# Column sums of the adaptive parameters between matmuls of an up group, and down groups that wait for their activation remainders by halves

## What is computed

```python
# end of the first block: the feed-forward part, D_FF = 2816
hf = rms_norm(x, g_pre_ffn)
f_gate, f_up = jnp.split(hf @ w_ffn_in, 2, axis=-1)
f = (jax.nn.silu(f_gate) * f_up) @ w_ffn_out
return x + rms_norm(f, g_post_ffn)

# start of each layer of the second block: 3072 adaptive parameters
c_act = jax.nn.silu(c)
mod = c_act @ w_ada + b_ada          # (1, 1024) @ (1024, 3072)
shift, scale, gate = jnp.split(mod, 3, axis=-1)
```

## Time and profile before

| | |
|---|---|
| median of 3 runs | 2731.32 us |
| profiled execution, its own time | 2728.5 us |
| its span | 2726.8 us |
| mean granted TensorE clock | 0.983 |
| TensorE busy | 2643.9 us (97%) |
| TensorE weight loads busy | 2217.8 us (81%) |
| VectorE, ScalarE, POOL busy | 1213.8, 965.2 and 410.3 us |

### The profile page before, as it was taken

How to read it: one execution, slowest core, us unless ns; L and a number is a source line. 1 busy time by engine, 2 the same in 40 slices (tenths; PEclk the granted TensorE clock), 3 DMA queues, 4 the chain that set the end, 5 groups by cost and what they waited for, 6 DMA issues and landing times.

```text
span 2726.8 us, 33510 instructions
## 1 busy us (share of the span) xinstructions
PE 2643.9 (97%) x13229; PEld 2217.8 (81%) x13245; DVE 1213.8 (45%) x1645; ACT 965.2 (35%) x1289; POOL 410.3 (15%) x428
## 2 busy tenths in 40 slices
PE   7999999999999999998999999999999999999998
PEld 7887778777888878786888888888888888888887
DVE  5435554744534765634433333443443333343435
ACT  6425454225324412213433332323253333322222
POOL 3104332200000100000301001321021001032300
PEclk9989999999999999999999999999999999999999
DMA  5210003222242554522222223122222222322122
GB/s 202 92 62 17 17 17 105 92 82 78 93 178 85 186 185 151 188 78 93 93 95 100 90 100 113 68 104 77 94 84 101 92 92 98 124 83 94 72 102 76
DMA packets 43592, 269.39 MB, mean 99 GB/s; under 512 B 5128, under 2 KB 5264, under 8 KB 16224
## 3 DMA queue, kind: packets, MB, share of 16 engines
q1 hardware_dynamic: 32080, 227.59, 23.3%
q0 software_dynamic: 11120, 39.27, 4.2%
q10 hardware_dynamic: 288, 1.05, 0.1%
HBM read 265.79 MB, written 2.10 MB: 98 GB/s over the span
## 4 chain that ended last, share of the span: by engine, by line
PE 65%; issue 23%; DVE 6%; POOL 4%; ACT 2%; DMA 1%; DVEq 0%; POOLq 0%; SPq 0%; ACTq 0%
PE PS L1888 63%; DVE w_split L1148 1%; POOL merged L586 1%; PE PS L2113 1%; POOL res_lo L580 1%; POOL res_hi L580 1%; ACT w_split L623 1%; POOL merged L525 1%; DMA raw<-in_weights 1%; DVE small L1446 1%; DVE R L1534 0%; DVE h_act L1156 0%; DVE ks_lo L1383 0%; PE PS L2335 0%; PE PS L1975 0%
## 5 line engine op out<-in xcount | busy, mean ns | idle before, releaser
L1888 PE MATMUL PS<-h_act,w_split 128*128 128x512 f32 (+1 forms) x5856 | 1271.2, 379 | 12.7 <-DVE w_split L1148 3.8
L1888 PEld LDWEIGHTS PS<-h_act,w_split 128*128 128x128 f32 x5856 | 1054.2, 190 | 215.0 <-issue 4.3
L1148 DVE TENSOR_TENSOR w_split<-raw,w_split 128x2048 fp32r<-128x2048 f32 x213 | 504.6, 2369 | 905.0 <-ACT w_split L623 888.2
L623 ACT ACTIVATE w_split<-raw 128x2048 fp32r<-128x2048 f32 x213 | 407.7, 1914 | 824.4 <-PE PS L1888 815.7
L1888 PE MATMUL PS<-w_split,h_act 128*128 128x512 f32 (+1 forms) x1728 | 410.8, 387 | 4.5 <-DVE w_split L1148 3.3
L1888 PEld LDWEIGHTS PS<-w_split,h_act 128*128 128x128 f32 x1728 | 314.1, 190 | 60.2 <-DVE w_split L1148 4.3
L1888 PE MATMUL PS<-y_act,w_split 128*128 128x512 f32 x1152 | 265.4, 391 | 2.2 <-DVE w_split L1148 2.2
L1888 PEld LDWEIGHTS PS<-y_act,w_split 128*128 128x128 f32 x1152 | 217.5, 189 | 47.8 <-DVE w_split L1148 2.6
L1888 PE MATMUL PS<-R 128*128 128x128 f32 (+3 forms) x896 | 190.3, 364 | 9.7 <-ACT R L1041 5.5
L1888 PEld LDWEIGHTS PS<-R 128*128 128x128 f32 x896 | 135.2, 201 | 42.6 <-issue 15.5
L1888 PE MATMUL PS<-w_split,res_hi 128*128 128x384 f32 x512 | 130.9, 336 | 0.0
(11 more groups left out here) (276 smaller groups left out, 2144.9 us busy)
## 6 DMA issues: line engine op xcount, KB each, us to landing
raw<-in_weights SPq DMA_DIRECT2D x213, 1024.0 KB, 4.8
R<-in_w_ada POOLq DMA_DIRECT2D x36, 512.0 KB, 5.0
gate_bc<-in_w_ada POOLq DMA_DIRECT2D x12, 512.0 KB, 4.9
R<-in_nsa_wk POOLq DMA_DIRECT2D x1, 2048.0 KB, 10.3
xres<-in_x POOLq DMA_DIRECT2D x1, 2048.0 KB, 10.8
R<-in_decay POOLq DMA_DIRECT2D x8, 256.0 KB, 3.3
out<-R SPq DMA_DIRECT2D x3, 512.0 KB, 2.6
xres<-in_x ACTq DMA_DIRECT2D x2, 512.0 KB, 4.0
```

Source lines behind the costliest of these rows:

```text
L623: act.activation(w_split[:, 0, half, :, :], raw[:, half, :, :], ACT.Copy).then_inc(w_hi, 1)
L1148: dve.tensor_tensor(w_split[:, 1, half, :, :], raw[:, half, :, :], w_split[:, 0, half, :, :].bitcast(F32), ALU.subtract).then_inc(w_lo, 1)
L1888: return pe.matmul(out, lhsT, rhs, start=start, stop=stop, skip_group_check=True)
```

## The change

A pair of down groups no longer waits for all its remainders first. Its first group waits for those of contraction tiles 0 to 3 ahead of its first half, and for the rest ahead of its second half. This is done in three places (two chunks and the last pair).

The 24 column matmuls of a chunk no longer stand in a block behind the down groups. They stand in the next up group (up group a of the second chunk, and `ffn_up0`), one behind each second matmul from the tenth on: behind matmuls 10, 12, ... 56 of the 96. They write bank 4, of set 1, which that up group does not use; what waits for VectorE's addition is now the up group after it, which uses set 1.

VectorE adds the columns (`ada_columns`) inside that up group, behind its `split_lo` of the next group's first half. Because `ada_acc` must not be written before TensorE has read it, the panel that stood ahead of that group's work now stands behind the addition. VectorE's two loops are now written out by the host, so that places can differ.

```diff
--- before.py
+++ after.py
@@ -172,7 +172,7 @@
     ("w_o", C(g=2, u0=1, u1=1, h=6, l=6)),
     ("norm2", C(u1=1, h=2 * KT, l=2 * KT)),
     ("ffn", 2, [("up", 2, [("a", C(g=1, u0=1, s=2, l=2)), ("b", C(g=1, u1=1, s=2, l=2))]),
-                ("down", C(g=2, u0=1, u1=1)), ("ada", C(u0=1))]),
+                ("down", C(g=2, u0=1, u1=1)), ("ada", C(u1=1))]),
     ("ffn_up0", C(g=1, u0=1, s=2, l=2)),
     ("ffn_up1", C(g=1, u1=1, s=2, l=2)),
     ("ffn_up2", C(g=1, u0=1, s=2, l=2)),
@@ -1626,8 +1626,9 @@
                       lambda part, kts: norm_lo(at("norm2"), V_G2, part, kts))
 
 
-            def up(own, c, S, y0):
+            def up(own, c, S, y0, between=lambda: None):
                 split_lo(c.g + 1, 0)
+                between()
                 for b in range(2):
                     tile = stage[:, 2 * S + b:2 * S + b + 1, :]
                     dve.wait_ge(staged, c.s + b + 1)
@@ -1664,11 +1665,23 @@
             dve.wait_ge(fo_zero, 1)
             dve.wait_ge(cond_ready, 1)
             dve.wait_ge(mod_in, 32)
-            with dve.Fori(0, 2) as ch:
-                with dve.Fori(0, 2) as i:
+            def ada_columns(ch):
+                dve.wait_ge(ada_ps, ch + 1)
+                cols = ada[:, ch:ch + 1, :]
+                dve.tensor_tensor(cols, cols, PS[:, 4:5, 0:ADA_COLS], ALU.add).then_inc(ada_ready, 1)
+                release(1, ada_ready, ch + 1)
+
+            for ch in range(2):
+                for i in range(2):
                     own = Chain(dve, own_ffn, 2 * ch + i, 8 + 2 * KT)
-                    ada_panel(own, ch, 2 * i)
-                    up(own, at("ffn.up.a", ch, i), 0, 4 * i)
+                    if ch and not i:
+                        def columns_panel():
+                            ada_columns(0)
+                            ada_panel(own, 1, 0)
+                        up(own, at("ffn.up.a", ch, i), 0, 4 * i, columns_panel)
+                    else:
+                        ada_panel(own, ch, 2 * i)
+                        up(own, at("ffn.up.a", ch, i), 0, 4 * i)
                     ada_panel(own, ch, 2 * i + 1)
                     up(own, at("ffn.up.b", ch, i), 1, 4 * i + 2)
                     own.end()
@@ -1679,14 +1692,13 @@
                         dve.sem_inc(ada_summed, 1)
                     add_down(at("ffn.down", ch), n, n)
                 own.end()
-                dve.wait_ge(ada_ps, ch + 1)
-                cols = ada[:, bass.ds(ch, 1), :]
-                dve.tensor_tensor(cols, cols, PS[:, 0:1, 0:ADA_COLS], ALU.add).then_inc(ada_ready, 1)
-                release(0, ada_ready, ch + 1)
-            modulation(0)
             own = Chain(dve, own_ffn2)
+
+            def second_columns():
+                ada_columns(1)
+                modulation(0)
             for n in range(3):
-                up(own, at(f"ffn_up{n}"), n % 2, 2 * n)
+                up(own, at(f"ffn_up{n}"), n % 2, 2 * n, lambda: None if n else second_columns())
             own = line
             c = at("ffn_down")
             first_gain, second_gain = [gains[:, GAIN_SLOT["post2"], n * W:(n + 1) * W] for n in range(2)]
@@ -2211,29 +2223,39 @@
             merged_group(c, 24)
             last_group(c.plus(C(g=1)), 0, Hr, at("norm2"), ROWS["norm2"])
             Yr = rows_of(y_act, block_rows)
+
+            def group_with_columns(c, ch):
+
+
+                for n, _ in enumerate(dense(c, 0, H)):
+                    col = n // 2 - 4
+                    if n % 2 == 0 or not 0 <= col < ADA_COLS:
+                        continue
+                    if col == 0:
+                        pe.wait_ge(set_free[1], at("ffn.ada", ch).u1)
+                        pe.wait_ge(ada_summed, ch + 1)
+                    ins = mm(PS[:, 4, col:col + 1], ada_acc[:, col // 4, col % 4 * P:(col % 4 + 1) * P],
+                             cf[:, C_ONE:C_ONE + 1], True, True)
+                    if col == ADA_COLS - 1:
+                        ins.then_inc(ada_ps, 1)
+
             for ch in range(2):
                 for i in range(2):
                     if ch == i == 0:
                         first_group(at("ffn.up.a", 0, 0), at("norm2"), ROWS["norm2"])
+                    elif i == 0:
+                        group_with_columns(at("ffn.up.a", ch, i), ch - 1)
                     else:
                         group(at("ffn.up.a", ch, i), 0, H)
                     group(at("ffn.up.b", ch, i), 1, H)
                 c = at("ffn.down", ch)
-                pe.wait_ge(act_lo, c.l)
-                for n in range(2):
-                    group(c.plus(C(g=n)), n, Yr, feat=False)
-
-                pe.wait_ge(set_free[0], at("ffn.ada", ch).u0)
-                pe.wait_ge(ada_summed, ch + 1)
-                for col in range(ADA_COLS):
-                    last = mm(PS[:, 0, col:col + 1], ada_acc[:, col // 4, col % 4 * P:(col % 4 + 1) * P],
-                              cf[:, C_ONE:C_ONE + 1], True, True)
-                last.then_inc(ada_ps, 1)
-            for n in range(3):
+                group(c, 0, Yr, feat=False, lows=(c.l - 4, c.l))
+                group(c.plus(C(g=1)), 1, Yr, feat=False)
+            group_with_columns(at("ffn_up0"), 1)
+            for n in (1, 2):
                 group(at(f"ffn_up{n}"), n % 2, H)
             c = at("ffn_down")
-            pe.wait_ge(act_lo, c.l)
-            group(c, 1, Yr, feat=False, kph=(4, 2))
+            group(c, 1, Yr, feat=False, kph=(4, 2), lows=(c.l - 2, c.l))
             last_group(c.plus(C(g=1)), 0, Yr, at("layer.norm", 0), ROWS["layer"], kph=(4, 2))
 
 
```

## The result

| | before | changed |
|---|---|---|
| median, first comparison | 2730.34 us (4 runs, 2726.47 to 2734.41) | 2710.69 us (4 runs, 2709.37 to 2712.84) |
| profiled execution | 2728.5 us | 2711.64 us |
| its span, mean clock | 2726.8 us, 0.983 | 2709.9 us, 0.986 |

The ratio is 0.9929, with a 95% interval from 0.9911 to 0.9946. On 2730.34 us that is 19.4 us less, 14.7 to 24.3. The forecast was 2714.9 us: 16.4 less than the 2731.3 that it set out from, and 15.4 less than this median.

What follows compares the result with a forecast made beforehand. TensorE, busy 97% of the span, was taken to bound the kernel. Removing 6.46 + 16.00 + 4.88 = 27.3 us and adding 10.9 saves 16.4, so 2731.3 becomes 2714.9 us; range 2708 to 2724.

Steps and rivals of the forecast that it cites:

- The entry waits: TensorE's three waits for `y_act` at the entries of down group pairs; all 2.21 + 2.20 + 2.05 = 6.46 us goes.
- The blocks and the clock behind them: Two column blocks behind down groups: 16.00 us removed, plus 4.88 us lost to the lowered clock in wide matmuls behind.
- The price of a column: Columns among wide matmuls of the up groups: 0.226 us each, 10.9 us added in all.
- the lower bound of 0.107: Columns in the up groups: one exposed weight load each, 0.107 us, or 5.1 us added in all.
- The loops: VectorE's loops written out: they save VectorE its branch and add none on TensorE; 0 us.
- VectorE's timetable: Up group with columns, from its start T: next group's weight halves ready at T + 19.7 and about T + 32.5.
- The slack at the second: Next group's second weight half: ready at about T + 32.5, wanted at T + 38.1, T being the column group's start.
- A: Up groups with columns: the clock falls there too, 10.3 us lost in all, gain 6.1, 2725.2 us; chance 0.08.
- B: Down groups still wait at entry for hidden weights or banks; gain 9.9 us, 2721.4 us; chance 0.06.
- C: Up groups with columns: a column costs 0.77 us, 37.0 in all; 9.7 us slower, 2741.0 us; chance 0.04.

Runs made afterwards that it cites:

- The block inside the up group: Changed kernel with all 24 columns of a chunk as one block behind matmul 10 of the same up group; timed ratio to the kernel before 0.9949.
- one pass: Changed kernel with each column sum as one instruction of two equal columns, the panel's last addition rounded to the one-pass format; ratios to before 0.9917 and 0.9908.
- the second pair of traces: The kernel before and the changed kernel, each run once more unaltered for a second trace; spans 2730.1 and 2708.8 us.

## Why the prediction was right

- **The entry waits** went in full, and nothing took their place, for the reasons given (weights and remainders ready long before). The term was too small: 6.46 us against about 7.2. A bracket counts from the modelled end of the row before it, and where nothing waits the next row starts some 0.16 us ahead of that end (981.75 + 43.68 against 1025.27 in the changed kernel), so a gap costs that much more than its bracket; and the matmuls behind it run 0.1 to 0.2 us slower. The term left out that such a gap can lower the clock (1.6 us where it did).
- **The blocks and the clock behind them** were read rightly as one cost, 16.0 + 4.9 us. The block inside the up group shows the cause: short work alone, without a gap. How long half level lasts varies from block to block, 6.8 or 10.3 us.
- **The price of a column**, read from the attention stage, was 0.226 us against 0.233: 11.2 us in all, not 10.9. Taking it from 128-column neighbours was sound, since width hardly counts and the number of short instructions does, as one pass (0.124) suggests. One reading beside it was wrong. The Trainium skill ("TensorE: Matmul & The Clock Gate", "Step-by-step: what each phase is for") says that a weight load can be pulled ahead of a matmul in flight, and the prediction took from this that only one load a column would show, 5.1 us in all. It saw in the rows that something of the load behind the short ones shows too, and counted that against the page; but the load of the wide matmul behind has only a short one to hide beneath, so by the page's own rule it shows. At the block's 0.107 us a load that makes, as an estimate, 0.107 for a column of one instruction and 0.215 for one of two; measured are 0.124 and 0.233. So the trace agrees with that page, and the lower bound of 0.107 left out one load of two.
- **The loops** were priced at 0; they were worth the 0.37 us wait ahead of the first up group.
- **VectorE's timetable** was 1.4 us too early at the first weight half and 1.7 at the second: I left out the table load of 1.28 us ahead of ScalarE's split. The slack at the second was 3.9 us and not 5.6, still enough.
- The sum of the measured terms is 7.2 + 16.0 + 4.9 + 0.4 - 11.2 = 17.3 us, against 17.4 in the stretch and 16.4 forecast. The spans of the two profiled executions differ by 16.9. That the sum comes so close is in part luck: the entries (0.7) and the loops (0.4) were priced too low as gains, the columns (0.3) too low as a cost, and these partly cancel.
- **The rivals.** A (half clock in the mixed stretch) failed at three spacings of the columns. The Trainium skill's warning of a kernel that goes round its PSUM banks ("TensorE: Matmul & The Clock Gate", "A second HAM failure mode: psum-queue depth-cycling") did not come true here: the clock is at 1.00 in all three. B (entries still wait) and C (a column at 0.77 us) failed as well.
- **What stays open.** The medians differ by about 20 us, the stretch by 17.4. The interval, 14.7 to 24.3, holds both. The profiled execution of before was 1.8 us faster than the median of its four runs and that of the changed kernel 1.0 us slower. In the second pair of traces the spans differ by 21.3 us, and there the surplus lies outside the stretch, mostly in half clock behind it, and not at an entry. Whether that is so in most executions of the kernel before, and whether the change has a part in it, was not seen.

## What to carry to other kernels

A stretch of short matmuls costs TensorE its own time and, once the clock has fallen, time in the wide matmuls behind it; add both before judging what a move is worth. Short work spread among wide matmuls keeps its own price, per short instruction, and saves the rest. Where an engine's wait names several conditions at once, ask which of them the first instructions behind it need.

## What the runs showed of the hardware beside that

- A gap of 2.05 to 2.2 us between wide matmuls lowered the clock to 1.2 GHz for some 3.4 us at two of three entries in one kernel and at one of three in another, and at none in two traces of a third; it costs 1.6 us where it comes.
- An unbroken block of 48 short matmuls lowered the clock to 1.2 GHz with no gap beside it, 3.4 and 4.2 us after its start in the two chunks, for 6.8 us; in the block with a wait behind it the clock fell 2.3 to 5.2 us after the start, for 6.8 or 10.3.
- The price of a short matmul among wide ones hardly depends on the mix: 0.233 us for two instructions behind two wide ones, 0.226 behind one, 0.231 in blocks of eight columns.
